# The gated recurrence woven between the spans of eighteen projection chunks, and a query norm carried in the softmax scale

## The reference, cut to what matters

```python
def _odd_mixer(h, pos, s0, kbuf, vbuf, lb, w_in, w_out, onorm_g, qn_g, kn_g, sinks):
    qc, fc, ic, gc, qd, kd, vd = _split(h @ w_in, ODD_SIZES)      # 4x512, 512, 128, 128 columns
    f = lb + (1.0 - lb) * jax.nn.sigmoid(fc)
    q_c = jax.nn.silu(qc)
    o_c, s_new = _hgrn2(q_c, 1.0 - f, jnp.log(f), ic, s0)          # 4 heads, state 128 x 128
    o_c = _rms_norm(o_c, onorm_g) * jax.nn.silu(gc)
    q_d = _rope(_rms_norm(qd, qn_g), pos, ROT_DIM_D, ROPE_THETA)   # 8 query heads of 64
    k_d = _rope(_rms_norm(kd, kn_g), pos, ROT_DIM_D, ROPE_THETA)   # 2 key heads
    o_d, k_new, v_new = _swa_prompt(q_d, k_d, vd, sinks)           # window 128, softmax with a sink
    y = jnp.concatenate([o_c, o_d], axis=-1) @ w_out
```

## Time and profile before

| what | value |
|---|---|
| median of 3 runs | 3347.86 us (3347.75 to 3349.96) |
| profiled execution | 3348.07 us, span 3346.3 us, mean granted TensorE clock 0.943 |
| PE busy | 3069.6 us, 92% |
| DVE busy | 1559.3 us, 47% |
| POOL busy | 1059.2 us, 32% |
| ACT busy | 531.4 us, 16% |

### The profile page before, as it was taken

One profiled execution on the slowest core, in us unless ns is written; L12 is line 12 of the kernel. 1 busy time (PEld: TensorE's weight loads), 2 busy tenths in 40 slices (PEclk: granted clock), 3 DMA queues, 4 the chain that ended last, 5 costly groups with the idle time before them and its releaser, 6 DMA issues. The chain is left out here.

```text
span 3346.3 us, 43932 instructions
## 1 busy us (share of the span) xinstructions
PE 3069.6 (92%) x18135; PEld 2921.8 (87%) x18135; DVE 1559.3 (47%) x1786; ACT 531.4 (16%) x874; POOL 1059.2 (32%) x551
## 2 busy tenths in 40 slices
PE   7997769999999999999988879689989999999999
PEld 6987558889999999998987768469879999999999
DVE  4152454357626436256114545663446635526343
ACT  3111122152000000002111021350252000000000
POOL 3332033213334344343320132103203434344342
PEclk9998679999999999999986789789999999999999
DMA  3111121311111111113100121011231111111112
GB/s 118 45 32 38 24 91 51 114 63 54 39 49 44 39 49 41 47 38 100 42 19 14 47 62 33 15 68 49 81 112 50 42 46 44 43 46 44 44 44 81
DMA packets 274509, 175.86 MB, mean 53 GB/s; under 512 B 15262, under 2 KB 261406, under 8 KB 274398
## 3 DMA queue, kind: packets, MB, share of 16 engines
q1 hardware_dynamic: 274398, 174.29, 17.1%
HBM read 158.00 MB, written 16.27 MB: 52 GB/s over the span
## 5 line engine op out<-in xcount | busy, mean ns | idle before, releaser
L327 PE MATMUL psum<-moving_hi,w_hi 128*128 128x384 f32 (+1 forms) x3888 | 1283.5, 330 | 72.3 <-PEq L515 24.9
L328 PE MATMUL psum<-moving_lo,w_hi 128*128 128x384 f32 (+1 forms) x3888 | 1277.6, 329 | 0.0
L329 PE MATMUL psum<-moving_hi,w_lo 128*128 128x384 f32 (+1 forms) x3888 | 1277.4, 329 | 0.0
L289 POOL TENSOR_TENSOR w_hi<-w_raw,one 128x1024 fp32r<-128x1024 f32 (+2 forms) x236 | 406.9, 1724 | 1908.2 <-PE psum L329 1464.9
L327 PEld LDWEIGHTS psum<-moving_hi,w_hi 128*128 128x128 f32 x3888 | 738.0, 190 | 80.6 <-issue 61.9
L328 PEld LDWEIGHTS psum<-moving_lo,w_hi 128*128 128x128 f32 x3888 | 738.3, 190 | 0.5 <-issue 0.5
L329 PEld LDWEIGHTS psum<-moving_hi,w_lo 128*128 128x128 f32 x3888 | 737.8, 190 | 0.0
L294 POOL TENSOR_TENSOR w_lo<-w_raw,w_hi 128x1024 fp32r<-128x1024 f32 (+2 forms) x236 | 575.2, 2437 | 18.5
L368 DVE TENSOR_TENSOR residual<-psum,residual 128x768 f32 x192 | 130.1, 719 | 490.5 <-PE psum L329 489.9
L327 PE MATMUL psum<-hidden_hi,w_hi 128*128 128x384 f32 (+1 forms) x1056 | 344.6, 326 | 3.2 <-DVE hidden_lo L1900 3.2
L329 PE MATMUL psum<-hidden_hi,w_lo 128*128 128x384 f32 (+1 forms) x1056 | 345.1, 327 | 0.0
(11 more groups left out here) (292 smaller groups left out, 2849.0 us busy)
## 6 DMA issues: line engine op xcount, KB each, us to landing
w_raw<-in_ffn_w_gate SPq DMA_DIRECT2D x44, 512.0 KB, 3.8
w_raw<-in_ffn_w_up SPq DMA_DIRECT2D x44, 512.0 KB, 3.8
w_raw<-in_ffn_w_down SPq DMA_DIRECT2D x48, 384.0 KB, 3.1
w_raw<-in_od_w_in SPq DMA_DIRECT2D x22, 512.0 KB, 3.9
w_raw<-in_ev_w_in SPq DMA_DIRECT2D x20, 512.0 KB, 3.7
w_raw<-in_mem_w_kv SPq DMA_DIRECT2D x16, 512.0 KB, 3.6
work_h<-in_cache_mem_kT SPq DMA_DIRECT2D x4, 2048.0 KB, 8.6
work_h<-in_cache_mem_v SPq DMA_DIRECT2D x4, 2048.0 KB, 13.2
```

The lines of the kernel that those rows point to most:

```text
L289: nc.gpsimd.tensor_tensor(hi, raw, ONE.to_broadcast([P, kt * P]), ALU.mult).then_inc(own.sem, 1)
L327: pe.matmul(out, sh, mh, start=(k == 0), stop=False)
L328: pe.matmul(out, sh, ml, start=False, stop=False)
L329: return pe.matmul(out, sl, mh, start=False, stop=(k == kt - 1))
```

## The change

The three blocks of query, forget and gate projections, the block of the local attention's projections and `hgrn` become one block, `project_and_recur`. It has 18 chunks in a new order, `MIXED`: q0 f0 q1 f1 q2 f2 q3 f3, key, value, four local query tiles, g0 to g3. Every chunk uses PSUM banks 0 to 2 and each span has its own semaphore. PE's order is 54 steps, one span each; in steps 7 to 46 a span is followed by one round of the recurrence. Banks 3 and 4 hold scores, 5 to 7 the pieces of the head before, and from step 40 on banks 3 and 4 take the sums of five norms (the key tile and four heads). `grow` moves from POOL to DVE. The state loads and stores move from SP's queue to ACT's, as two loads and three stores a head.

```diff
-    run(g.project, ws[0][0], HHL, KT, 4, To(R, 0, func=ACT.Silu, times=INV), then=ws[1], meanwhile=...)
-    run(g.project, ws[1][0], HHL, KT, 4, To(R, 4, func=ACT.Sigmoid, times=INV))
-    run(hgrn)
-    run(g.project, ws[3][0], ... norm=(g.ONES128[:, :], ...)), then=w_qkv, loads=swa_loads, zero=(...))
-    run(g.project, w_qkv[0], HHL, KT, 6, To(tiles=qk + [V], times=INV, norm=(g.ONES64, ...)), then=out)
-    run(g.turn_rows, ...)
-    run(g.rotate, qk, [H[:, 6, :], H[:, 7, :]])
-    run(spread_queries)
+    MIXED = [(what, h) for h in range(HEADS) for what in "qf"] + [("k", 0), ("v", 0)] + [("s", i) for i in range(4)] + [("g", h) for h in range(HEADS)]
+    run(g.project, ic[0], ..., then=(pick_mixed, CHUNKS), lead=..., early=Early(tables, lower_peak_and_share, lower_exp))
+    run(project_and_recur)
+    run(prepare_attention)
```

```diff
-                if x.scales is not None:
+                if x.scales is not None and x.sink is not None:
+                    dve.tensor_tensor(nm, mx, x.scales[1], ALU.mult).then_inc(dve_own.sem, 1)
+                    dve.wait_ge(dve_own.sem, dve_own.next())
+                    dve.tensor_tensor(nm, nm, x.sink, ALU.min).then_inc(dve_own.sem, 1)
+                    dve.wait_ge(dve_own.sem, dve_own.next())
+                    last = dve.tensor_tensor(df, nm, x.sink, ALU.subtract)
+                elif x.scales is not None:
...
-        return Unit(P, 4, W, ..., mask, SINK[:, 4 * s:4 * s + 4])
+        return Unit(P, 4, W, ..., mask, SINK[:, 4 * s:4 * s + 4], (SCALE[:, j, s, :], NEGATIVE[:, j, s, :]))
```

More of the change, by code:

```diff
@@ L1982, in _layer1, with pick_mixed @@
+    AT = {"q": 0, "f": 4, "g": 12, "s": 16, "k": 20, "v": 21}
+    CHUNKS = len(MIXED)
+    def pick_mixed(c, s, i):
+        what, x = MIXED[c]
+        return g.chunk(w_in, KT, AT[what] + x), KT
+    run(g.project, ic[0], HHL, KT, 4, To(OT, times=INV, rows=IC), then=(pick_mixed, CHUNKS), lead=Lead([X[:, k, :] for k in range(KT)], gain=0, inv=INV, spill=True, summed=True),
+        early=Early(tables, lower_peak_and_share, lower_exp))
     for c in (peaked, exped):
         c.adds(1)
-    CHAIN, S0 = view(g.Wf, 3 * T, NBLK, P), view(g.Wf, 3 * T + 1024, NB, P)
@@ L2161, in sample_states, with invert @@
                     last.then_inc(s_in.sem, 1)
[L2162 to L2173 removed]
+                def invert(x, half):
+                    root, a = ROOTS[x % 2], 544 * half
+                    dve.wait_ge(rooted.sem, rooted.at(3 * x + 2 + half))
+                    dve.reciprocal(root[:, a:a + 544], root[:, a:a + 544]).then_inc(dve_own.sem, 1)
+                    dve.wait_ge(dve_own.sem, dve_own.next())
@@ L2201, in _ @@
+                load_states(0)
+                for s in range(3 * CHUNKS):
+                    c = s // 3
+                    if s % 3 == 2 and MIXED[c][0] in "qfg":
+                        activate(c)
+                    h, k = step(s + 1)
+                    if h is not None and h < HEADS and k == 0:
+                        prepare(h)
+                    h, k = step(s)
+                    if h and k == 1:
                         take_keys(h - 1)
-                    if h + 1 < HEADS:
-                        prepare(h + 1)
@@ L2272, in _layer1 @@
-    run(g.project, ws[3][0], HHL, KT, 4, To(OT, 4, func=ACT.Silu, times=INV, into=[OT[:, h, :] for h in range(4)], heads=[OT[:, h, :] for h in range(4)],
-        norm=(g.ONES128[:, :], [COL[:, 12 + h:13 + h] for h in range(4)], 4, R[:, 10, :], R[:, 11, :])), then=w_qkv, loads=swa_loads,
-        zero=(VC[:, :, 0, 64:128], VC[:, :, 1, 0:64], VD[:, :, 0, 64:128], VD[:, :, 1, 0:64], QZ))
-    run(g.project, w_qkv[0], HHL, KT, 6, To(tiles=qk + [V], times=INV,
-        norm=(g.ONES64, [COL[:, 36:37]] * 4 + [COL[:, 37:38]], 5, R[:, 10, :], R[:, 11, :])), then=out)
@@ new lines, in _ @@
+                for j in range(NBLK):
+                    last = dve.tensor_scalar(VAR[:, j], sums[:, j], XM[:, j:j + 1], None, ALU.add)
+                last.then_inc(varied.sem, 1)
+                dve.wait_ge(s_rooted.sem, s_rooted.at(1))
+                own(dve.reciprocal(VS, VS))
+                turn_tile(4)
+                dve.wait_ge(added.sem, added.at(5))
+                qs = OT[:, 4:8, SEQ:T]
+                own(dve.tensor_tensor(qs, qs, VS, ALU.mult))
+                dve.wait_ge(rooted.sem, rooted.at(1))
@@ L2289, in _ @@
+                own(dve.reciprocal(VAR, VAR))
+                dve.tensor_scalar(SCALE, VAR, 64 ** -0.5, None, ALU.mult)
+                dve.tensor_scalar(NEGATIVE, VAR, -64 ** -0.5, None, ALU.mult)
                 for bt in range(2):
@@ L2317, in prompt_unit @@
         mask = BAND[:, MEM - W:MEM].unsqueeze(1).to_broadcast([P, 4, W])
-        return Unit(P, 4, W, [(x, P) for x in range(0, W, P)], scores, outputs, place, j % 2, s == 0, s == 1, mask, SINK[:, 4 * s:4 * s + 4])
+        return Unit(P, 4, W, [(x, P) for x in range(0, W, P)], scores, outputs, place, j % 2, s == 0, s == 1, mask, SINK[:, 4 * s:4 * s + 4], (SCALE[:, j, s, :], NEGATIVE[:, j, s, :]))
     def sample_unit(bt, s):
```

488 lines of the change are left out of this document (340 added, 148 removed).

## The result

The changed kernel takes 3260.64 us (median of 4 runs, 3259.44 to 3263.89), the kernel before 3348.49 (3347.75 to 3349.96): a ratio of 0.9739, 95% interval 0.9722 to 0.9756, 87.9 us less. The forecast was 3268 (3244 to 3306). The profiled execution is the slowest of the four, 3263.89 for a span of 3262.1.

A forecast was written before the change was run, and what follows sets the result against it. PE was taken to set every projection's end, with neither PE nor DVE alone bounding the recurrence. The stretch of 500.2 us would become 417.2, plus 3.2 in the attention: saving 79.8, so 3348 - 80 = 3268 us, range 3244 to 3306.

The forecast's parts named there:

- the likeliest case: The forecast itself for the whole kernel: 3268 us, a saving of 79.8, given a chance of 0.56.
- Work of PE: PE's work in the fused block at full clock: chunks 213.3, four heads 109.6, norms 10.3, changes of matmul kind 8; 341.2 us.
- the 8 us for changes between kinds of matmul: In the block's 40 woven steps, PE loses 0.2 us each switching matmul kinds; bounds 0 and 16.
- The clock: In the fused block, a mean granted clock of 0.98 costs 8 us, bounds 0 and 35; under 0.93 the prediction is wrong.
- Rival 2: Clock falls in each head at sample outputs and narrow scores: 3295 us at mean 0.90, 3315 at 0.85; chance 0.15.
- Waits: PE waits 5.4 us ahead of three sample outputs and 7.3 before step 51; plain rounds cost nothing on DVE.
- Collisions: In the block, DVE updates meeting POOL's weight splits cost 3 us, bounds 0 and 20.
- The tail: At the block's end, DVE's queued work, Silu, the last gate product and five zeroings leave 15.3 us after PE.
- rival 3: DVE's chain becomes the bound because splits hit updates of rounds 2 to 4: 20 us more, 3285; chance 0.07.
- Rival 5: The weave gives nothing because PE waits for DVE each round anyway: price 56 us, 3324; chance 0.03.
- rival 4: Slower than before: the block at 1.2 GHz for most of its length, 3403 us at clock 0.69; chance 0.02.
- Rival 1: Nothing lost on the way: full clock, no collisions, free changes of work; 3244 us, about 3256 with half; chance 0.17.

The follow-up runs named there:

- Run 11: Run 10 without the eight products of 8 columns of each head's sample outputs: 3218.7 us.
- Run 7: The changed kernel with POOL's split for the tenth chunk waiting until DVE has masked head 2's diagonal: 3258.2 us.
- run 2: The changed kernel with DVE masking the scores ahead of chaining the states in round 2 of each head: 3253.4 us.
- Runs 9 to 11: First, the changed kernel with gate products and zeroings earlier, mask before chain, `grow` behind the diagonal's mask: 3236.5 us; then Run 10 and Run 11.
- run 1: The changed kernel with POOL multiplying the first two gate products ahead of its last two splits, not after: 3255.3 us.
- run 6: The changed kernel with the minimum with the sink done twice in each unit of the attention: 3266.6 us.
- Run 10: The first kernel of Runs 9 to 11, with `grow` ahead of the diagonal's mask again for head 0 alone: 3233.1 us, ratio 0.9653.
- run 5: The changed kernel with all forty recurrence rounds bunched in one step, score ahead of the piece and mask ahead of the chains: 3376.5 us.

## Why the prediction was right, step by step

The time came out 7 us under the forecast and inside the likeliest case. Half of the 7 are small terms (block 0.8, preparation 1.6, attention 0.8, `ic` 0.4 less than foretold); the other half is that the median lies 3.3 under the profiled execution that these are read from. The waits of PE came where they were foretold. But two terms of the sum were mis-sized by 10 us each, in opposite directions, and the tail (3 too much) and waits that were not foretold (3 too little) in the same way: that they cancel is luck.

**Work of PE: too high.** I had 341.2. Run 11 shows the woven part at full clock: 322.8 busy, and 8 for the products it lacks, 331. The term that fails is the 8 us for changes between kinds of matmul. From 1698.76 to the next take at 1704.06 there are 5.30 us for a span of 3.51 and a score costed at 2.0: the score cost 1.8, not 2.2. There is no charge for switching here; the lower bound, 0, was the value. Another 2 us are spread over the terms.

**The clock: too low a price.** I took 8; PE was busy 348.8 us in the block, 18 more than the 331. The mean was 0.94, just above the 0.93 that I had named as the mark of a wrong prediction. Rival 2's mechanism did happen, at half its price, and the surplus of work covered it. The falls come where rival 2 put them, at sample outputs and narrow scores, and one more behind the collision. In the Trainium skill (TensorE: Matmul & The Clock Gate, HAM oscillation — how this bites in real kernels) only idle gaps bring the clock down. Run 7 agrees, and run 2 for two of its three gaps: with the gap its fall went. Runs 9 to 11 don't, since falls stay where PE never idled and go with the 8-column products. The measurement decides, and my reading of the earlier trace rows was not wrong but only half of it.

**Waits.** Ahead of three sample outputs 5.5 (5.4 foretold), at step 51 7.5 (7.3), with DVE's wait for POOL 16.9 (15), and run 1 shows its cause. Plain rounds cost PE under 1 in all, as said. Not foretold: 2.9 at the transposes and 1.4 ahead of an output product.

**Collisions: the right size, the wrong picture.** I took 3 us, spread over a fifth of the updates. Updates meet splits (one took 2.88 at 1688.90, in place of 0.69) and are absorbed; the 2.9 come from one operation with no slack, `grow` in the round of the diagonal, which I had called hidden beside the scores. It costs its clock as well, since a fall of about 10 us follows (0.57 from 1784 to 1796). The rule of the Trainium skill (SBUF — State Buffer, Who interferes with whom), that a DVE operation with two SBUF inputs and one of POOL that reads SBUF exclude each other, fits the rows: 2.22 us without POOL, 5.75 beside it. Its price here is set by where the one long meeting falls, not by the count of splits; rival 3's 20 us didn't come.

**The tail**: 12.1 against 15.3. Silu's table was in place before its last take, so 1.1 stood there, not 2.4; and DVE's queued work ended 2 us sooner than I had it. Block: 379.4 against 380.2, by 331 of work, 18.6 of waits, 18 of clock and 12.1 of tail, to within a microsecond.

**Around it.** `ic` cost at most 0.6 (1 taken): the block starts at 1628.9, where it was 1628.3. `prepare_attention` took 34.4 (36); DVE's tiles, five of about 4.0, set its pace from the third on, and PE's first matmuls ran at the lower clock, as said. `_attend`: units 5.87 apart, where they were 5.67, 2.4 in all (3.2); run 6 shows the price of one such operation directly.

**Rivals.** Rival 5 is out, since PE waits for DVE under 1 us in all the plain rounds, and rival 4, since the block ran at 0.94 (by its own terms its 3403 should have read 3413: 3268 + 494 - 341 - 8). Rival 1 came true only in its free changes of work: the clock fell and one collision cost 2.9. Run 10 gets below its 3244, to 3233, with four changes of order and no other, because they take away waits that rival 1 had kept.

## What to carry to other kernels

Weave a chain of small dependent steps between long matmuls of another job, one step to a span: it fills the gaps and holds the clock, and the second was half of the gain here. Then list, engine by engine, what stands ahead of each instruction that the bound engine waits for; changes of order alone, with the same operations, were worth 28 us, a third as much again as the change. A longer wait that a span hides costs nothing until the span is gone: `score`'s wait for one more mask is free in the weave and cost 26 us in the bunched rounds of run 5. A gap costs more than its length where narrow matmuls follow it: three gaps of 5.5 us in all were worth 7 to 9.

## What the hardware showed that I had not expected

- A gap on PE of 1.97 us ahead of 8-column products was followed by a fall from 2.4 GHz to 1.2 for about 10 us (0.57 from 1733 to 1745); the same products with no gap ran at 2.4 GHz there, and elsewhere the clock fell behind them after 10 us without any gap (run 10, 0.57 from 1858 to 1866). Neither the gap nor the busy share tells alone when it falls.
- Taking one fall away can lengthen the next: about 7 us became about 10 in run 7.
- Changing between spans, 64-column scores and transposes costs PE nothing that these traces show: a span of 3.51 and a score took 5.30 between takes, and with nine transposes and a ninth block of scores more, 6.67 (1716.93 to 1723.60).
- Six dependent products of DVE that lasted 2.2 us alone lasted 5.75 beside two POOL operations of 1.90 and 2.75: DVE lost 3.5 of POOL's 4.65 us.
